# Attention with four score banks and norming behind the value product, feed-forward accumulators without zero products

## The reference, cut to what matters

```python
# both attentions, per head and block of 128 queries, 512 keys (256 context, 256 own)
s = q @ k.T * scale            # na: plus bias and mask on the own keys
p = softmax(s)
o = p @ v
# every layer, after its mixer
x = x + g1 * (o @ w_out)
x = x + g2 * (act(h @ w1) * (h @ w3)) @ w2      # layer 2: width-3 convolution inside act
```

## Time and profile before

| what | value |
|---|---|
| median of 3 runs | 1272.9 us (1269.86 to 1273.78) |
| profiled execution, its own time | 1279.1 us |
| its span, first to last instruction | 1276.9 us |
| PE busy | 1172.0 us, 92% of the span |
| DVE busy | 802.0 us, 63% |
| ACT busy | 648.9 us, 51% |
| POOL busy | 368.3 us, 29% |
| mean granted TensorE clock | 0.936 of full speed |
| DMA | 232.82 MB, mean 182 GB/s |

### The profile page before, as it was taken

The page is one execution under the profiler, slowest core; times in us unless marked ns, Lnnn a source line. Parts: engine busy times, 40 slices in busy tenths (PEclk is TensorE's granted clock), DMA queues, the critical chain, the costliest instruction groups (busy, mean ns, idle before and its releaser), DMA issues.

```text
span 1276.9 us, 21844 instructions
## 1 busy us (share of the span) xinstructions
PE 1172.0 (92%) x8548; PEld 1045.0 (82%) x8548; DVE 802.0 (63%) x1116; ACT 648.9 (51%) x1116; POOL 368.3 (29%) x259
## 2 busy tenths in 40 slices
PE   5787997989999987889899999899999889999998
PEld 1575864889999985669899999888875559999998
DVE  0682657577666658976867676634515876766664
ACT  2363456566655647636655656422324555544452
POOL 2241713524544407612254455300001312000000
PEclk9787887989999979999799999799898898999999
DMA  8656313557777735766287787422320203555550
GB/s 328 257 213 246 116 38 111 208 179 266 269 279 267 243 131 205 268 262 238 96 291 259 266 285 250 144 67 83 132 100 21 66 22 130 193 176 189 181 181 33
DMA packets 68156, 232.82 MB, mean 182 GB/s; under 512 B 12096, under 2 KB 12256, under 8 KB 67712
## 3 DMA queue, kind: packets, MB, share of 16 engines
q1 hardware_dynamic: 62064, 227.27, 50.2%
q0 software_dynamic: 5888, 3.73, 1.0%
q10 hardware_dynamic: 144, 1.05, 0.2%
HBM read 230.91 MB, written 1.05 MB: 182 GB/s over the span
## 4 chain that ended last, share of the span: by engine, by line
PE 71%; DVE 18%; ACT 5%; issue 3%; DMA 2%; SPq 0%; DVEq 0%; ACTq 0%
PE bank L1325 21%; PE bank L1326 20%; PE bank L1327 20%; DVE vals L1219 4%; DVE w_lo L930 3%; DVE h_lo L982 2%; DVE big L973 2%; PE bank L1348 2%; PE bank L1368 1%; PE bank L1452 1%; PE bank L1736 1%; DMA con<-consts 1%; PE bank L1399 1%; DVE bank L995 1%; PE bank L1376 1%
## 5 line engine op out<-in xcount | busy, mean ns | idle before, releaser
L1325 PE MATMUL bank<-h_hi,w_hi 128*128 128x256 f32 (+1 forms) x1648 | 493.4, 299 | 23.9 <-DVE h_lo L982 15.3
L1326 PE MATMUL bank<-h_lo,w_hi 128*128 128x256 f32 (+1 forms) x1648 | 485.3, 294 | 0.0
L1327 PE MATMUL bank<-h_hi,w_lo 128*128 128x256 f32 (+1 forms) x1648 | 484.7, 294 | 0.0
L930 DVE TENSOR_TENSOR w_lo<-w_raw,w_hi 128x1024 fp32r<-128x1024 f32 x281 | 407.5, 1471 | 115.0 <-ACT w_hi L575 114.6
L1325 PEld LDWEIGHTS bank<-h_hi,w_hi 128*128 128x128 f32 x1648 | 323.5, 196 | 41.2 <-issue 20.3
L1326 PEld LDWEIGHTS bank<-h_lo,w_hi 128*128 128x128 f32 x1648 | 324.4, 197 | 4.0 <-issue 0.2
L1327 PEld LDWEIGHTS bank<-h_hi,w_lo 128*128 128x128 f32 x1648 | 323.9, 197 | 4.3
L575 ACT CAST w_hi<-w_raw 128x1024 fp32r<-128x1024 f32 x281 | 288.9, 1044 | 58.8 <-PE bank L1327 46.0
L507 POOL TENSOR_TENSOR a_raw<-a_raw,bias 128x1024 f32<-128x1024 f32 x88 | 223.8, 2550 | 310.6 <-DMA a_raw<-ada 310.5
L1325 PE MATMUL bank<-g_hi,w_hi 128*128 128x256 f32 x528 | 149.9, 284 | 4.9 <-DVE g_lo L1076 4.7
L1326 PE MATMUL bank<-g_lo,w_hi 128*128 128x256 f32 x528 | 148.9, 282 | 0.0
(11 more groups left out here) (146 smaller groups left out, 1291.8 us busy)
## 6 DMA issues: line engine op xcount, KB each, us to landing
w_raw<-weights SPq DMA_DIRECT2D x281, 512.0 KB, 4.2
a_raw<-ada SPq DMA_DIRECT2D x144, 512.0 KB, 5.4
bias<-rpb POOLq DMA_DIRECT2D x16, 224.0 KB, 7.3
xT<-xt SPq DMA_DIRECT2D x1, 1024.0 KB, 10.0
big<-ctx SPq DMA_DIRECT2D x1, 1024.0 KB, 12.0
big<-ctx ACTq DMA_DIRECT2D x1, 1024.0 KB, 4.7
out_t<-xT SPq DMA_DIRECT2D x2, 512.0 KB, 2.6
con<-consts SPq DMA_DIRECT2D x1, 999.0 KB, 13.5
```

Source lines behind the costliest of these rows:

```text
L930: nc.vector.tensor_tensor(w_lo[:, s, :], w_raw[:, s, :], w_hi[:, s, :].bitcast(fp), SUB)\
L1325: nc.tensor.matmul(out, a_hi, b_hi, start=start, stop=False)
L1326: nc.tensor.matmul(out, a_hi, b_lo, start=False, stop=False)
L1327: return nc.tensor.matmul(out, a_lo, b_hi, start=False, stop=stop)
```

## The change

Attention: the score tiles rotate over banks 0, 1, 7 and 6, and PE runs two steps ahead with them. `prob` is transposed as it comes from the exponential. The reciprocals of four row sums are taken at once; behind a pair's last value product PE spreads them with four small products over the other half of the output bank. ACT copies the output to `o_unit` (it reuses `ada_s`), DVE multiplies it by the spread half (`out_normed`), and cast and low part are taken from `o_unit`. ACT does the exponential first and the copy of tile n-2 behind it. Feed-forward: the zero products and `zero_r` go; turn 0 and turn 10 are written out around the loop, the first product of a bank opens it and the last closes it; DVE adds bank by bank behind a new semaphore `acc_done`.

```diff
 place_attention
-                place_tile((name, "sc", n), (0, 1, 7)[n % 3], (exp_ready, at0 + n + 1))
+                place_tile((name, "sc", n), (0, 1, 7, 6)[n % 4], (exp_ready, at0 + n + 1))
-                place_tile((name, "o", p), 4 + p % 2, (o_lo, o0 + p + 1), (pv_done, at0 + 4 * (p + 1)))
+                place_tile((name, "o", p), 4 + p % 2, (o_normed, at0 // 4 + p + 1))
 ACT, attention
+                def out_copied(p):
+                    b = wait_tile(act, (name, "o", p))
+                    if p >= 2:
+                        act.wait_ge(o_lo, o0 + p - 1)
+                    nc.scalar.copy(o_unit[:, p % 2, :], b[:, 0:T]).then_inc(o_copied, 1)
                 def out_hi(p):
-                    b = wait_tile(act, (name, "o", p))
-                    nc.scalar.copy(h_hi[:, p, 0:T], b[:, 0:T]).then_inc(o_hi, 1)
+                    act.wait_ge(o_normed, at0 // 4 + p + 1)
+                    nc.scalar.copy(h_hi[:, p, 0:T], o_unit[:, p % 2, :]).then_inc(o_hi, 1)
-                        if n >= 2:
-                            turned(n - 2)
                         ... (exponential of n)
+                        if n >= 2:
+                            turned(n - 2)
+                    if j >= 4 and j % 2 == 0:
+                        out_hi(j // 2 - 2)
                     if j >= 3 and j % 2:
-                        out_hi((j - 3) // 2)
+                        out_copied(j // 2 - 1)
 DVE, attention
+                def row_sums(p):
+                    dve.wait_ge(exp_ready, at0 + 4 * (p + 1))
+                    nc.vector.reciprocal(rinv[:, 4 * p:4 * (p + 1)], rsum[:, 4 * p:4 * (p + 1)]).then_inc(rinv_ready, 1)
+                def out_normed(p):
+                    b = wait_tile(dve, (name, "o", p))
+                    dve.wait_ge(o_copied, at0 // 4 + p + 1)
+                    nc.vector.tensor_tensor(o_unit[:, p % 2, :], o_unit[:, p % 2, :], b[:, T:2 * T], MUL).then_inc(o_normed, 1)
+                maximum(0)
+                maximum(1)
                 for j in range(heads):
-                    for n in (2 * j, 2 * j + 1):
-                        maximum(n)
-                    for n in (2 * j, 2 * j + 1):
-                        dve.wait_ge(exp_ready, at0 + n + 1)
-                        step(nc.vector.reciprocal(rinv[:, n:n + 1], rsum[:, n:n + 1]))
-                        nc.vector.tensor_scalar(prob[:, n % PROBS, :], prob[:, n % PROBS, :], rinv[:, n:n + 1], None, MUL)\
-                            .then_inc(prob_ready, 1)
+                    if j + 1 < heads:
+                        maximum(2 * j + 2)
+                        maximum(2 * j + 3)
+                    if j % 2:
+                        row_sums(j // 2)
                     ... (a weight split in steps 1 to 4)
+                    if j >= 3 and j % 2:
+                        out_normed(j // 2 - 1)
+                    if j >= 4 and j % 2 == 0:
+                        out_lo(j // 2 - 2)
 PE, attention
-                    pe.wait_ge(prob_ready, at0 + n + 1)
+                    pe.wait_ge(exp_ready, at0 + n + 1)
+                    if t == 1:
+                        pe.wait_ge(rinv_ready, at0 // 4 + p + 1)
+                        for n in range(4):
+                            e, t = n % 2, n // 2
+                            ins = nc.tensor.matmul(b[e * VH:(e + 1) * VH, T + t * P:T + (t + 1) * P],
+                                                   rinv[:, 4 * p + n:4 * p + n + 1].broadcast_to([P, VH]), ident,
+                                                   start=True, stop=True)
+                        ins.then_inc(full_of((name, "o", p)), 1)
                 scores(0)
+                scores(1)
                 for j in range(heads):
-                    if j + 1 < heads:
-                        scores(j + 1)
+                    turn(2 * j)
+                    turn(2 * j + 1)
+                    if j + 2 < heads:
+                        scores(j + 2)
                     if j:
                         weigh(j - 1)
-                    turn(2 * j)
-                    turn(2 * j + 1)
 PE, ffn
-                for b4 in range(4):
-                    b = write_tile(pe, ("acc", layer, b4))
-                    for q4 in range(4):
-                        nc.tensor.matmul(b[:, q4 * P:(q4 + 1) * P], zero_r[:, :], zero_r[:, :], start=(q4 == 0),
-                                         stop=False)
+                        for j in range(KT):
+                            ins = down_tile(s, j, start=isinstance(i, int) and i == 0, stop=last)
+                            if last and s == 1 and j % 2 and j < KT - 1:
+                                ins.then_inc(acc_done, 1)
-                with pe.Fori(0, FT // 2 - (layer == 2)) as i:
+                turn(0)
+                with pe.Fori(1, FT // 2 - 1) as i:
                     turn(i)
-                if layer == 2:
-                    turn(FT // 2 - 1, splits_on=False)
-                for b4 in range(4):
-                    ... (16 closing products of zeros)
+                turn(FT // 2 - 1)
```

More of the change, by code:

```diff
@@ L292, in program @@
         stored = sem("stored")
+        acc_done = sem("down_bank_done")
         tiles, last_taken, made_count = {}, [None] * 8, [0] * 8
@@ L1026, in attention @@
                     if j >= 3 and j % 2:
-                        out_lo((j - 3) // 2)
+                        out_normed(j // 2 - 1)
+                    if j >= 4 and j % 2 == 0:
+                        out_lo(j // 2 - 2)
+                out_lo(heads // 2 - 2)
+                out_normed(heads // 2 - 1)
                 out_lo(heads // 2 - 1)
@@ L1103, in ffn @@
                 wait_mods(dve, 12 * (layer + 1))
-                for b4 in range(4):
-                    b = wait_tile(dve, ("acc", layer, b4))
-                    for e in range(2):
-                        j = 2 * b4 + e
-                        nc.vector.scalar_tensor_tensor(out=xT[:, j, :], in0=b[:, e * T:(e + 1) * T],
-                                                       scalar=mods[:, layer, 5 * KT + j, 0:1], in1=xT[:, j, :],
-                                                       op0=MUL, op1=ADD).then_inc(x_updated, 1)
+                for j in range(KT):
+                    b, made, _ = tiles["acc", layer, j // 2]
+                    if j < KT - 2:
+                        dve.wait_ge(acc_done, (KT // 2 - 1) * layer + j // 2 + 1)
+                    else:
+                        dve.wait_ge(*made)
+                    nc.vector.scalar_tensor_tensor(out=xT[:, j, :], in0=bank[b][:, (j % 2) * T:(j % 2 + 1) * T],
+                                                   scalar=mods[:, layer, 5 * KT + j, 0:1], in1=xT[:, j, :],
+                                                   op0=MUL, op1=ADD).then_inc(x_updated, 1)
             nc.vector.memset(bank[6][:, :], 0.0).then_inc(ada_cleared, 1)
@@ L1526, in up, with down_ready, down_tile @@
                             ins.then_inc(w_used, 1)
-                    def down(s):
-                        w = w0 + 4 + s
-                        pe.wait_ge(split_done, 6 * i + (w + 1))
+                    def down_ready(s):
+                        pe.wait_ge(split_done, 6 * i + (w0 + 4 + s + 1))
                         pe.wait_ge(ff_lo, 2 * i + (g0 + s + 1))
-                        for j in range(KT):
-                            b = bank[tiles[("acc", layer, j // 2)][0]]
-                            a = wtile(w, j * P, P)
-                            out = b[:, (j % 2) * T:(j % 2 + 1) * T]
-                            ins = split3(out, a[0], a[1], g_hi[:, s, :], g_lo[:, s, :], False, False)
-                        ins.then_inc(w_used, 1)
+                    def down_tile(s, j, start=False, stop=False):
+                        if start and s == 0 and j % 2 == 0:
+                            write_tile(pe, ("acc", layer, j // 2))
+                        b = bank[tiles[("acc", layer, j // 2)][0]]
+                        a = wtile(w0 + 4 + s, j * P, P)
+                        return split3(b[:, (j % 2) * T:(j % 2 + 1) * T], a[0], a[1], g_hi[:, s, :], g_lo[:, s, :],
+                                      start and s == 0 and j % 2 == 0, stop and s == 1 and j % 2 == 1)
@@ L1539, in turn @@
                     up(0)
                     up(1)
-                    down(0)
-                    down(1)
-                with pe.Fori(0, FT // 2 - (layer == 2)) as i:
-                    turn(i)
-                if layer == 2:
-                    turn(FT // 2 - 1, splits_on=False)
-                for b4 in range(4):
-                    name = ("acc", layer, b4)
-                    for q4 in range(4):
-                        ins = nc.tensor.matmul(bank[tiles[name][0]][:, q4 * P:(q4 + 1) * P], zero_r[:, :], zero_r[:, :],
-                                               start=False, stop=(q4 == 3))
-                    ins.then_inc(full_of(name), 1)
+                    last = isinstance(i, int) and i == FT // 2 - 1
@@ new lines, in turn @@
```

(10 more changed lines are left out.)

26 lines of the change are left out of this document (13 added, 13 removed).

## The result

The changed kernel takes 1232.3 us (median of 4 runs, 1224.27 to 1235.61) beside 1271.4 us for the kernel before on the same chip (1267.72 to 1273.78). The ratio is 0.9686, 95% interval 0.9632 to 0.9739, or about 40 us less. The direction was as forecast; the gain is larger than the forecast's 24.7 us and lies outside its range. Timed a second time beside other kernels it gave 1234.4 us and a ratio of 0.971 (0.968 to 0.9739).

A forecast was written before the change was run, and what follows sets the result against it. PE, busy 92%, was taken to bound the feed-forward loops, with time to win in attention and feed-forward ends; -9.7 - 8.3 + 0.9 - 2.2 - 2.2 - 2.8 - 0.4 = -24.7 us, 1272.9 to 1248.2 us, range 1239 to 1260.

The forecast's parts named there:

- At the full clock one step of na takes PE 2.15 us for two score tiles ... I take 4.1 us of PE for a step: na attention: PE's own work 65.6 us; with spreading products, start and last copies 70.6 in place of 80.3, -9.7 us.
- mla: forecast -8.3: mla attention: ideal 34.9 us of PE work, but 218.5 as its end in place of 226.8; bounds -13.1 and -4.
- The two things "in the way": mla: POOL's scaling of four blocks slows DVE's instructions, and ACT's last steps take some 3.9 us each.
- Behind mla: +0.9: After mla: ACT's extra copy, cast and two handovers delay the second context's load; +0.9 us, all exposed.
- Feed-forward ends: -2.2, -2.2, -2.8: Ends of layers 0, 1, 2: without closing zero products DVE's sums start earlier; -2.2 us each, and -2.8 in layer 2.
- The feed-forward starts: -0.4: Layers 0 and 1 gain nothing; in layer 2 PE starts 1.5 us earlier but DVE's parts pace it, -0.4 us.
- One sign of being wrong: Behind a norm: a stretch with no products longer than before by more than 1.7 us would show the forecast wrong.
- the 1.7 us set against them: Feed-forward starts: without zeros the clock could rise later, costing up to 1.7 us at each of three starts.
- The lockstep: Rival, attention: PE waits for ACT and ACT for the spread in every odd step; -10 us, 1263; chance 0.05.
- a low clock without a pause before it: Sign of a rival, attention: transposes and narrow products do not hold the full clock; slower, case at 1277; chance 0.04.
- Rival 3: The low clock goes too, in mla, na and both norms: -33 us, 1240; chance 0.13.
- Only the waits shift: Rival: mla gives 4, na 6, the ends 1.5 each, layer 2's start loses 1.7; -14 us, 1259; chance 0.17.

The follow-up runs named there:

- the kernel with the attention part alone: The changed kernel with its feed-forward changes undone, zero products back in place: 1240.0 us, ratio 0.9753 to the kernel before.
- the later moves: Added to the changed kernel: na's first score tiles earlier, second context load earlier, DVE scaling four blocks instead of POOL, in several combinations; medians 1226.5 to 1230.3 us.
- the part's own timing: The kernel before with only the feed-forward changes, attention untouched: 1261.5 us, ratio 0.9907, which is 7 to 16 us less.

## Why the prediction failed, by its own steps

**The step that failed: "At the full clock one step of na takes PE 2.15 us for two score tiles ... I take 4.1 us of PE for a step".** The 2.15 us were read as PE's own price. They were 1.06 us of product for two tiles at once, or 1.92 one behind the other, and the rest a wait for a bank, hidden because PE's records of the first tile ran on meanwhile. PE's floor with the spread is 3.33 us a step and not 4.36. The sum had 70.6 us for na; 16 x (4.36 - 3.33) = 16.5 us come off that, which leaves 54.1. 58.5 were measured: the rest of the window over 16 steps of 3.33 is 5.2 us, where I took 0.9 for the start and the last copies. Of these 5.2 PE is idle for 3.26 (58.50 - 55.24), and it ran at the low level (1.2 GHz) for 3.4 us, from 951.3 to 954.8, behind the pauses of 1.56 and 0.59 us, which is another 1.7. It was a term of the sum that was mis-sized, not the mechanism. PE was forecast to become the slowest engine of na, and it did, with 36.36 of 37.00 us busy. Before the change 16 steps of 3.16 us (1.06 + 1.03 + 1.07) were PE's own work, so that some 30 of the 80.3 us were waiting and low clock, and not 14.7. The fourth bank, for which the forecast gave no price of its own, is worth 4.0 us there; without the relief it gave 2.9 in na and nothing that can be told in the kernel.

**mla: forecast -8.3, measured -11.4.** Again PE's floor. Two tiles of 96 rows without a wait between take 1.81 us (the row behind this one begins at 190.21), about what na's two take on one half, so that they do not overlap as na's do; but that is still less than the 2.15 of the forecast:

```profile
188.40 1.88 PE L1477 MATMUL bank<-big 96*128 96x512 f32 x4
```

PE's step with the spread is some 4.0 us and not 4.36 (from 184.63 to 192.60 two steps took 7.97): 3 us in eight steps. The two things "in the way" were there. The collision is measured at 3.3 us. I had taken `out_lo` for harmless, since only the projection reads it; it stands in DVE's queue ahead of the maxima, and that was the wrong question to ask. The rule of the Trainium skill that the prediction weighed (SBUF — State Buffer, "Who interferes with whom") gave up to 2.4 us of waiting for it; 2.57 us in place of 0.43 agree.

**Behind mla: +0.9, measured +1.3** (+1.4 in the second profile). The chain is as described. Before, ACT issued the load of the context 0.15 us behind mla's last product (226.95 against 226.80), after the change 1.41 us behind it:

```profile
215.59 0.37 ACTq L836 DMA_DIRECT2D big<-ctx  x1
```

ACT's wait for it stayed the same, 4.40 and 4.43 us, so the +1.3 is the later issue behind ACT's two additional steps: 0.37 us for the copy and 0.92 of waiting for DVE's multiply. Issued early, the load is waited for no more and the stretch falls by 1.9 us.

**Feed-forward ends: -2.2, -2.2, -2.8, measured -5.0, -3.0 and -2.5 in one pair of profiles.** The first sum does start right behind DVE's last split, as forecast (at 440.84, with no wait before it), and the norm's sums behind layer 0 took 2.36 us and not 4.40:

```profile
443.48 2.36 PE L1424 MATMUL bank<-con,big 128*128 128x1 f32 x20 [1.54 <-ACT big L632]
```

That shorter time is not the change's own, since the kernel with the attention part alone has it with its zero products in place; part of the 5.0 us is luck of the pair of profiles. Over more profiles, three with zero products and six without them and without the later moves, layer 0 took 207.8 us on average (206.6 to 208.9) against 204.3 (203.1 to 205.5), layer 1 211.8 against 209.8, layer 2 202.3 against 199.7 with its start. That is 3.5 + 2.0 + 2.6 = 8.1 us, against the forecast's 7.6, and the part's own timing (7 to 16) does not contradict it.

**The feed-forward starts: -0.4, measured nothing.** In layer 2 products begin 2.62 us behind the norm's spread and not 3.78, but they run at the low level for longer. Windows of both kernels, from the first products on, the kernel before first:

```profile
1079.00:1083.00 4.00, 4.00 (x23) 4.00 (x23) 3.02 (x8) 3.10 (x7) 0.00 (x0) 0.59 0.00 0
1083.00:1087.00 4.00, 4.00 (x36) 4.00 (x35) 2.83 (x5) 2.19 (x3) 0.00 (x0) 1.00 0.18 48
```

```profile
1033.60:1038.00 4.40, 4.40 (x17) 4.11 (x18) 4.40 (x12) 3.00 (x7) 0.00 (x0) 0.50 0.00 0
1038.00:1042.00 4.00, 4.00 (x28) 4.00 (x27) 2.02 (x3) 3.31 (x5) 0.00 (x0) 0.74 0.02 4
```

A mean of 0.59 over 4 us is 3.3 at the low level, and 0.74 is 2.1. So the full clock (2.4 GHz) came back at about 1082.3, 7.5 us behind the norm's spread, before, and at about 1040.1, 9.1 us behind it, after. PE began its 96th product there 16.84 us behind the spread before and 17.31 after, so the low stretch took back more than the head start of 1.2 us. But neither lasts: 20.35 us behind the spread PE needs DVE's `g_lo`. It waited 0.39 us for it before, and 0.89 us in the kernel with the attention part alone, where the zero products are in place and the clock stayed at 1.00; in the changed kernel it comes just in time (20.33):

```profile
1095.16 0.36 PE L1325 MATMUL bank<-g_hi,w_hi 128*128 128x256 f32 x1 [0.39 <-DVE g_lo L1076]
```

```profile
1056.12 0.35 PE L1348 MATMUL bank<-g_hi,w_hi 128*128 128x256 f32 x1 [0.89 <-DVE g_lo L1099]
```

From there on all three run alike (the 480th product began 63.39, 63.39 and 63.37 us behind the spread). The forecast had DVE's `h_lo` as the pace and missed this wait, which makes the start worth nothing either way.

One sign of being wrong that the prediction named did come: stretches without products behind a norm, zero products counted as such, became longer by more than 1.7 us, in layer 1 (from none to 3.46 us) and in layer 2 (from none to 1.91), and in layer 0 by 1.2. In layer 0 the clock was low for 10.2 us behind the norm's spread and not for 6.8. It cost none of the three starts the 1.7 us set against them: in layers 0 and 1 the 96th product began 0.4 and 0.6 us earlier than before.

**The rivals.** The lockstep did not come: no PE wait returns in the odd steps. Nor did a low clock without a pause before it: 1.00 over 37 us of transposes, value products and overlapped scores, about 1.03 of each 3.33 us in transposes. Rival 3, the low clock gone in both attentions and the norms, lies nearest by its number (1240), which is luck; na's clock is 0.97 and mla's 0.95, and the missing time is in the tiles. *Only the waits shift* is ruled out by mla and na, which gave 11.4 and 21.8 us.

## What to carry to other kernels

A row of products without idle time before it is not a price. Look at the weight loads beside it: where they come in two groups with a wait between, the row holds a wait, and a spot where the same products follow one another unheld (here the first three tiles of na, 1.98 us for three) gives the true one. Products with 64 rows on different halves of the partitions are worth placing next to each other, in different banks, with both banks free at that moment. And before costing an instruction by who reads its result, ask who stands behind it in its queue.

## What the runs showed of the hardware that had not been expected

Two fp32 score tiles of 64 rows and 512 columns took 1.06 us together on two halves of the partitions and 1.92 us on one half, at the full clock. With the second tile let in late, the same two took 1.32, 1.59 or 2.22 us, and PE counted as busy all the while. Two tiles of 96 rows took 1.81 us. A subtraction of 128x256 with two SBUF operands took 2.57 us with POOL's scaling beside it and 0.43 without.
